# A hybrid attention and PEER layer on one core: the products' columns walked from last to first

## The reference

```python
# token mixing
p = rmsnorm(x) @ w_in                         # 4096 -> 5456 columns, split into 20 parts
o_a = stick_breaking_attention(...)           # four heads
o_b = dsa_attention(...)                      # indexer picks the top 64 keys
o_c = nsa_attention(...)                      # compressed, selected, window
o_d = dilated_attention(...)                  # three dilations
z = rmsnorm(x) @ gate_down
merged = sum(sigmoid(z @ gate_up[i]) * (o_i @ w_branch_i) for i in range(4))
h = x + merged @ w_out
# PEER channel mixing
q = rmsnorm(h) @ peer_wq
s1, s2 = q1 @ subkeys[:, 0], q2 @ subkeys[:, 1]     # top 16 of 64 each, then top 16 of 256 pairs
out = h + (weights(top 16 of 4096 experts) * gelu(rmsnorm(h) @ u.T)) @ v
```

## Time and profile before

| what | us |
|---|---|
| median of 3 runs | 1908.49 |
| lowest and highest | 1908.01, 1910.51 |
| profiled execution, first to last instruction | 1906.1 |
| busy in it: PE, PEld | 1900.6, 1567.2 |
| busy in it: DVE, ACT, POOL | 1463.9, 984.9, 36.2 |

### The profile page before, as it was taken

How to read it: one execution, slowest core, us unless ns; L and a number is a source line. 1 busy time by engine, 2 the same in 40 slices (tenths; PEclk the granted TensorE clock), 3 DMA queues, 4 the chain that set the end, 5 groups by cost and what they waited for, 6 DMA issues and landing times.

```text
span 1906.1 us, 25847 instructions
## 1 busy us (share of the span) xinstructions
PE 1900.6 (100%) x8941; PEld 1567.2 (82%) x8941; DVE 1463.9 (77%) x2139; ACT 984.9 (52%) x1214; POOL 36.2 (2%) x49
## 2 busy tenths in 40 slices
PE   9999999999999999999999999999999999999999
PEld 8888888888888888888888888888887788888887
DVE  7578775584556889889765555899988878999897
ACT  6653644445456655546454464444444455555553
POOL 0010010000000000000000000000000000000000
PEclk9999999999999999999999999999999999999999
DMA  9976666655655668877887776767766668666664
GB/s 326 344 226 166 172 174 199 176 156 157 191 177 178 185 190 288 278 226 238 254 256 234 216 226 218 232 208 221 219 201 198 197 208 290 223 213 218 210 219 155
DMA packets 198832, 412.69 MB, mean 217 GB/s; under 512 B 45792, under 2 KB 124256, under 8 KB 198080
## 3 DMA queue, kind: packets, MB, share of 16 engines
q1 hardware_dynamic: 174048, 369.35, 63.0%
q10 hardware_dynamic: 20976, 25.19, 3.9%
q0 software_dynamic: 3696, 16.65, 2.4%
HBM read 390.15 MB, written 20.97 MB: 216 GB/s over the span
## 4 chain that ended last, share of the span: by engine, by line
PE 97%; DVE 2%; DMA 0%; issue 0%; ACT 0%; SPq 0%; DVEq 0%; ACTq 0%
PE acc L676 25%; PE acc L679 25%; PE acc L683 25%; PE acc L724 3%; PE acc L726 3%; PE acc L730 3%; PE side L1039 1%; PE side L1038 1%; PE acc L1152 1%; PE side L1040 1%; PE acc L1079 1%; PE acc L1085 1%; PE side L854 1%; PE acc L1080 1%; PE side L966 1%; DVE w_lo L1608 1%
## 5 line engine op out<-in xcount | busy, mean ns | idle before, releaser
L1608 DVE TENSOR_TENSOR w_lo<-w_raw,w_hi 128x1024 fp32r<-128x1024 f32 (+1 forms) x649 | 785.6, 1214 | 389.7 <-ACT w_hi L1199 384.9
L1199 ACT ACTIVATE w_hi<-w_raw 128x1024 fp32r<-128x1024 f32 (+1 forms) x649 | 681.1, 1052 | 701.2 <-PE acc L683 577.5
L676 PE MATMUL acc<-w_hi,xt_hi 128*128 128x512 f32 x1348 | 365.7, 393 | 0.0
L679 PE MATMUL acc<-w_hi,xt_lo 128*128 128x512 f32 x1348 | 360.8, 390 | 0.0
L683 PE MATMUL acc<-w_lo,xt_hi 128*128 128x512 f32 x1348 | 360.6, 389 | 0.0
L679 PEld LDWEIGHTS acc<-w_hi,xt_lo 128*128 128x128 f32 x1348 | 253.1, 188 | 53.1
L683 PEld LDWEIGHTS acc<-w_lo,xt_hi 128*128 128x128 f32 x1348 | 253.1, 188 | 52.9
L676 PEld LDWEIGHTS acc<-w_hi,xt_hi 128*128 128x128 f32 x1348 | 250.2, 188 | 51.5 <-issue 1.8
L676 PE MATMUL acc<-w_hi,x_hi 128*128 128x512 f32 x640 | 175.1, 396 | 0.0
L679 PE MATMUL acc<-w_hi,x_lo 128*128 128x512 f32 x640 | 171.5, 390 | 0.0
L683 PE MATMUL acc<-w_lo,x_hi 128*128 128x512 f32 x640 | 171.4, 390 | 0.0
(11 more groups left out here) (376 smaller groups left out, 2061.5 us busy)
## 6 DMA issues: line engine op xcount, KB each, us to landing
w_raw<-in_stream SPq DMA_DIRECT2D x504, 512.0 KB, 4.2
w_raw<-in_w_in SPq DMA_DIRECT2D x16, 496.0 KB, 4.1
w_raw<-in_w_in SPq DMA_DIRECT2D x16, 480.0 KB, 3.9
w_raw<-in_w_in SPq DMA_DIRECT2D x16, 464.0 KB, 3.8
w_raw<-in_w_in SPq DMA_DIRECT2D x16, 448.0 KB, 3.9
w_raw<-in_w_in SPq DMA_DIRECT2D x16, 432.0 KB, 3.9
w_raw<-in_w_in SPq DMA_DIRECT2D x16, 416.0 KB, 4.0
w_raw<-in_w_in SPq DMA_DIRECT2D x16, 400.0 KB, 3.8
```

The costliest lines, as they stand in the source:

```text
L676: pe.matmul(o[h], lhs(k0 + j, h)[0], wh[j], start=first and j == 0, stop=False)
L679: pe.matmul(o[h], lhs(k0 + j, h)[1], wh[j], start=False, stop=False)
L1199: nc.scalar.activation(w_hi[:, slot, 0:width], w_raw[:, slot, 0:width], ACT.Copy).then_inc(hi_ready, 1)
L1608: nc.vector.tensor_tensor(w_lo[:, slot, 0:width], w_raw[:, slot, 0:width], w_hi[:, slot, 0:width].bitcast(F32), ALU.subtract).then_inc(lo_ ...
```

## The change

A helper `back(row)` returns `row[:, ::-1]`. It is put around every moving operand and around every accumulator of the fp32r products, in `products`, `first_products`, `branch_products`, `ring`, `fast_products`, `last_products` and `plain_products`. Both patterns get the step -1 and start at their last column, so column c of the weights still goes to column c of the accumulator, only in the order 511, 510, ..., 0 (or from 335 or 255 down). The stationary operands, the data in SBUF and PSUM, the order and number of the instructions, all waits and all the small matmuls are as they were. The patterns start and end at multiples of four elements, before and after.

```diff
+            def back(row):
+                return row[:, ::-1]
...
-                wh = [w_hi[:, slot, j * width:(j + 1) * width] for j in range(2)]
-                wl = [w_lo[:, slot, j * width:(j + 1) * width] for j in range(2)]
-                o = [acc[:, parity, h, 0:width] for h in range(NT)]
+                wh = [back(w_hi[:, slot, j * width:(j + 1) * width]) for j in range(2)]
+                wl = [back(w_lo[:, slot, j * width:(j + 1) * width]) for j in range(2)]
+                o = [back(acc[:, parity, h, 0:width]) for h in range(NT)]
...
-                    o = acc[:, 0, h, :]
+                    o = back(acc[:, 0, h, :])
...
-                return [[w[:, slot, j * 512:(j + 1) * 512] for j in range(2)] for w in (w_hi, w_lo)]
+                return [[back(w[:, slot, j * 512:(j + 1) * 512]) for j in range(2)] for w in (w_hi, w_lo)]
...
-                t = [[w[:, i // 2, i % 2, :] for i in range(4)] for w in t_tiles[pair in OUT_PAIRS][1:]]
-                c11, c21, c12 = (acc[:, pair_bank(pair, i), h, :] for i, h in ((0, 0), (0, 1), (1, 0)))
+                t = [[back(w[:, i // 2, i % 2, :]) for i in range(4)] for w in t_tiles[pair in OUT_PAIRS][1:]]
+                p1, p5, p6, p7 = (back(side[:, i, :]) for i in range(4))
+                c11, c21, c12 = (back(acc[:, pair_bank(pair, i), h, :]) for i, h in ((0, 0), (0, 1), (1, 0)))
...
-                    o = side[:, side_n, 0:256]
+                    o = back(side[:, side_n, 0:256])
...
-                    o = acc[:, pair_bank(pair, i), h, :]
+                    o = back(acc[:, pair_bank(pair, i), h, :])
```

More of the change, by code:

```diff
@@ L688, in first_products @@
                 pe.wait_ge(hi_ready, chunk + 1)
-                wh = [w_hi[:, slot, j * width:(j + 1) * width] for j in range(2)]
-                wl = [w_lo[:, slot, j * width:(j + 1) * width] for j in range(2)]
-                k0, o = 2 * chunk, [acc[:, 0, h, 0:width] for h in range(NT)]
+                wh = [back(w_hi[:, slot, j * width:(j + 1) * width]) for j in range(2)]
+                wl = [back(w_lo[:, slot, j * width:(j + 1) * width]) for j in range(2)]
+                k0, o = 2 * chunk, [back(acc[:, 0, h, 0:width]) for h in range(NT)]
                 for j in range(2):
@@ L714, in branch_products @@
                 pe.wait_ge(hi_ready, chunk + 1)
-                wh = [w_hi[:, slot, j * 512:(j + 1) * 512] for j in range(2)]
-                wl = [w_lo[:, slot, j * 512:(j + 1) * 512] for j in range(2)]
+                wh = [back(w_hi[:, slot, j * 512:(j + 1) * 512]) for j in range(2)]
+                wl = [back(w_lo[:, slot, j * 512:(j + 1) * 512]) for j in range(2)]
                 for h in range(NT):
@@ L1065, in from_t @@
                         if d == 0:
-                            thrice(side[:, 1, :], s_tile[0], t, 0, first, last)
-                            thrice(side[:, 3, :], s_tile[2], t, 1, first, last)
-                        else:
-                            thrice(side[:, 2, :], s_tile[1], t, 2, first, last)
-                of_ring = ((side[:, 0, :], xt(2 * kp, 0), wa, 0, first), (c11, xt(2 * kp + 1, 0), wa, 1, opens),
+                            thrice(p5, s_tile[0], t, 0, first, last)
+                            thrice(p7, s_tile[2], t, 1, first, last)
+                        else:
+                            thrice(p6, s_tile[1], t, 2, first, last)
+                of_ring = ((p1, xt(2 * kp, 0), wa, 0, first), (c11, xt(2 * kp + 1, 0), wa, 1, opens),
                            (c12, s_tile[3], wb, 1, opens))
@@ L1115, in last_products @@
                     cols = slice(side_n * 256, side_n * 256 + 256)
-                    o = side[:, side_n, 0:256]
+                    o = back(side[:, side_n, 0:256])
                     for j in range(2):
-                        wh, wl = (w[:, slot, j * 512:(j + 1) * 512][:, cols] for w in (w_hi, w_lo))
+                        wh, wl = (back(w[:, slot, j * 512:(j + 1) * 512][:, cols]) for w in (w_hi, w_lo))
                         xh, xl = xt(2 * kp + j, 1)
```

## The result

The changed kernel takes 1955.8 us (median of 4 runs, 1955.4 to 1955.9), the kernel before 1908.9 in the same comparison. The ratio is 1.0245, with a 95% interval of 1.0233 to 1.0258: 2.45% slower, 47 us. The profiled execution's span is 1953.5 us, 47.4 more than before.

The account below looks back on a forecast made before the run. PE was taken to bound the kernel, by matmul count times distance between starts. All terms were 0, so 8073 products added 0 to the 1906.1 us span; with the runs' 2.4 us above it, 1908.5 us, range 1832 to 1937.

Parts of the forecast that it names:

- What bounds the kernel: Whole kernel: PE holds 97% of the chain, DVE 2%; time is a count times the distance between matmul starts.
- Moving operand, "I take 0": fp32r products: reading moving columns from last to first costs 0, within bounds from 0 to half the rate, 203 ns more.
- Accumulator, 0: fp32r products: writing PSUM from last to first costs 0, with half the rate, 430 ns, as upper bound.
- The fixed 13.4 ns: Every fp32r product: 13.4 ns beside its columns whatever the width, 10 ns of it for fp32r at full rate; change taken as 0.
- The 10 ns for each product behind 1835: fp32r products: reversal gives back at best 10 ns of the fixed cost, down to 1835 us; chance 0.14.
- The bound upwards, 4 ns from rows 9: Fixed cost of fp32r products: at most 4 ns more, from the first 512-wide products at 230.8 ns each.
- Half the rate: Rival, fp32r products: columns are taken two per step only when ascending; 203 ns more at 512 columns, 3531 us; chance 0.19.
- A few cycles for each product: Rival, fp32r products: a start at the high end costs up to 4 ns each, 28 us, 1937 us; chance 0.09.
- What would show it: 336-wide group: goes to 282 ns with half the rate, moves as much as the wide products with a fixed cost.

Follow-up runs that it names:

- e9: Changed kernel, but 16-byte groups of four columns ascend and only the four within each are reversed, in moving operand and accumulator; 1908.2 us, ratio 0.9998.
- e10: Changed kernel, but groups of four columns go from last to first while the four within each ascend; 1955.8 us, ratio 1.0249.
- e1: Changed kernel with only the moving operand read from last to first, accumulators written ascending; 1956.1 us, ratio 1.0247.
- e6: Kernel before, all patterns ascending, rings w_hi and w_lo moved 32 bytes and the tiles behind them 64; 1953.1 us, ratio 1.0232.
- e2: Changed kernel with only the accumulators written from last to first, moving columns read ascending; 1908.3 us, ratio 0.9998.
- e15: Changed kernel with the four-series column order and rings moved 208 bytes, stationary operands 12 elements ahead of the ring; 1860.9 us, ratio 0.9748.
- e3: Bench without the layer, forty stretches of 60 matmuls, one pattern each: directions, starts, steps, widths; 226.7 ns forwards, 233.3 with the moving operand backwards.
- e16: Bench without the layer: eight column orders times sixteen stationary places in steps of 4 elements; lowest 220.0 ns, blocks of two in series 452 to 462.
- e8: Bench without the layer, 122 stretches of 80 matmuls: moving starts, ascending or descending blocks, widths; 226.9 ns for descending halves, 233.4 for descending groups of 4.
- e13: Bench without the layer: every second moving operand shifted, with the same or next matmul's stationary operand (228.3 to 231.8 ns); also four-series sequences (223.3 ns).
- e11: Bench without the layer, 81 stretches of 80 matmuls: interleaved series of blocks of 4 to 64 columns, and shorter weight loads; 223.3 ns up to 281.
- e5: Bench without the layer, 137 stretches of 80 matmuls: grid of moving starts against stationary shifts; 226.7 ns on the forward diagonal, 233.3 to 236.6 backwards.
- e12: Changed kernel with columns in four series, each taking every fourth group of four, in moving operand and accumulator; 1897.6 us, ratio 0.9942.
- e14: Four-series kernel with row tiles as outer and halves as inner loop in the plain products; 1896.4 us, ratio 0.9939.
- e4: Bench without the layer, 55 stretches of 160 matmuls: starts, directions, stationary shifts, widths of weight load; 226.7 ns forwards at start 0, none below 233.3 backwards.

## Why the prediction was wrong

- *What bounds the kernel*: right. The chain went from 97% to 100% on PE, and the time followed the count times the distance.
- *Moving operand, "I take 0"*: this is the step that failed. No row showed the 0 that the sum uses. Reversal inside groups of four columns did cost nothing (e9: 226.8 ns, ratio 0.9998), but the groups in descending order cost the whole (e10: 233.5 ns, ratio 1.0249). The term measured 6.6 ns for each product of 512 columns in a long stretch, and it is all of the 47 us (e1: 1956.1 us with the moving operand alone reversed). The reasoning also missed that the moving operand's place relative to the stationary one enters (e6: 45 us without any reversal).
- *Accumulator, 0*: right, though no row showed it (e2, ratio 0.9998). e2 shows the time, not the reason.
- *The fixed 13.4 ns*: I took them for a property of fp32r alone. They depend on order and place as well: the same product's 233.5, 226.8 and 220.0 ns in e10, e9 and e15 leave 20.1, 13.4 and 6.6 ns beside the prediction's 213.4 for 512 columns. The columns' part and the prediction's 2.4 GHz are estimates from the 0.418 ns a column of the earlier trace rows (1 / 0.418 = 2.39, with a column taken as a cycle); the views of these runs give the clock as a share only.
- *The 10 ns for each product behind 1835*: no run shows this term. Reversal gave nothing back at 512 columns (233.3 ns in place of 226.7 in e3), and what did bring the distance down was another order with another place (220.0 ns, 1860.9 us in e15).
- *The bound upwards, 4 ns from rows 9*: too low, and with it the range's end of 1937. Those rows were themselves a sign that the distance depends on something besides the instruction; products behind an interruption took 230.0 and 230.8 ns on average, between the two levels. The bound came from the nearest row and not from a reason.
- *Half the rate*: did not happen for a step of -1. It did for a step of 2 (453 ns in e3), which skips half of each 16-byte group, and for blocks of two in series (452 to 462 ns in e16), which visit each group twice.
- *A few cycles for each product*, the case nearest to the result, had 0.09, and its mechanism (a start at the high end, once per instruction) was not the true one: line 283 of e8 starts at column 448, at the high end of the row, takes blocks of 64 downwards that ascend within, and costs nothing (226.9 ns). Nearest in size is not nearest in mechanism.
- *What would show it*: the 336-wide group was to tell a price per instruction from one per column. It showed 1.7 ns and was neither. In the benches, at that width, the two directions do not differ (153.5 and 153.3 ns in e3), and why the layer shows 1.7 stays open.

## What to carry to other kernels

Where TensorE bounds a kernel with fp32r products, the distance between matmuls is not fixed by the width: at 512 columns it went from 220.0 ns up. With 512 columns read upwards, moving and stationary operands at the same place modulo 256 bytes were the safe choice here (226.6 to 227.5 ns in the benches, 226.8 in long stretches of the layer). Treat a distance above 0.418 ns for each column as something that a bench of orders and places may lower, and confirm it in the kernel: the four series at place 0 kept their gain only in parts of the layer. Other widths need their own bench, since the sign of the difference changes with the width (backwards 3.4 ns more at 480 columns and 2.2 ns less at 488, e8). A distance measured in one layout is no proof for another, even when instructions, counts and waits are equal. Every order of the accumulator that was tried at 512 columns was free (step -1: 227.0 ns in e3; ascending or in four series under a moving operand in four series: 223.3 in e13), so there the accumulator could follow the moving order.

## What the runs showed of the hardware

- fp32r products of 512 columns took 220.0 (e15), 226.7 (e3), 233.3 (e3) or 240.0 ns (e8), 6.6 or 6.7 apart, with averages between them in some stretches. Series of small blocks took up to 281 ns (e11), blocks of two 452 to 462 (e16).
- Moving start and stationary operand interact modulo 256 bytes in fp32r (e5: 226.6 to 227.1 ns at equal places, 229.0 to 234.4 elsewhere upwards; e6: 45 us). bf16 gave 215.8 and 215.9 ns for other moving starts and backwards (e5); plain float32 was tried only backwards (426.7 ns a matmul, 429.2 forwards).
- One order and place can have two steady distances: 223.3 and 226.7 ns for four series at place 0 (e12, e14).
- In the moving operand a step of -1 within 16 bytes was free (e9: 226.8 ns), 16-byte groups downwards within 256 bytes cost 6.6 ns for each matmul of 512 columns with both operands at one place (e8: 233.4 against 226.8), blocks of 256 bytes downwards nothing (e8: 226.9), and a step of 2 halved the rate (453 ns, e3). At 336 columns and fewer the direction changed the distance by under 2 ns, with either sign (1.7 more at 336 in the layer, 1.6 less at 256 in e4). In PSUM -1 was free (e2: ratio 0.9998).
- Open: which weight load the moving reads relate to (e13: 228.3 to 231.8 ns with a shift of either), by what unit, and what picks one of two steady distances.
